# Latent attention: where the causal mask is added, and the order of scores, transposes, exponentials and copies

## The reference, cut to what matters

```python
def one(args):                                   # one block of 128 rows
    q_blk, i = args
    s = jnp.einsum('bhqd,bhkd->bhqk', q_blk, k).astype(jnp.float32) * scale
    qpos = i * Q_BLOCK + jnp.arange(Q_BLOCK)
    s = jnp.where(kpos[None, :] <= qpos[:, None], s, neg)
    p = jax.nn.softmax(s, axis=-1).astype(v.dtype)
    return jnp.einsum('bhqk,bhkd->bhqd', p, v)
```

## Time and profile before

| | |
|---|---|
| median of 3 runs | 1805.03 us (1804.6 to 1806.43) |
| span of the profiled execution | 1807.1 us (it is this execution's only time) |
| TensorE busy | 1759.0 us, 97% of the span |
| VectorE, ScalarE, GpSimd busy | 1087.8, 698.0, 982.2 us |
| first and last turn of latent attention | 602 to 774 us |
| mean granted TensorE clock | 0.993 |

### The profile page before, as it was taken

One profiled execution on the slowest core, in us unless ns is written; L12 is line 12 of the kernel. 1 busy time (PEld: TensorE's weight loads), 2 busy tenths in 40 slices (PEclk: granted clock), 3 DMA queues, 4 the chain that ended last, 5 costly groups with the idle time before them and its releaser, 6 DMA issues.

```text
span 1807.1 us, 25034 instructions
## 1 busy us (share of the span) xinstructions
PE 1759.0 (97%) x8599; PEld 1467.8 (81%) x8599; DVE 1087.8 (60%) x1535; ACT 698.0 (39%) x1243; POOL 982.2 (54%) x554
## 2 busy tenths in 40 slices
PE   7999999999999899999999999999999999999998
PEld 7888888888888677788878888778888888878887
DVE  5655663002334778884345564887777777889842
ACT  7422223111013667731133232644444444444432
POOL 6743333445654577654433232577777777655540
PEclk9999999999999999999999999999999999999999
DMA  6511111347661789583221134243433334494322
GB/s 266 204 52 36 36 43 49 139 164 256 227 227 46 276 317 325 177 308 113 103 71 59 59 104 141 77 139 107 142 117 123 133 110 139 142 344 143 122 76 93
DMA packets 111245, 262.33 MB, mean 145 GB/s; under 512 B 7744, under 2 KB 50368, under 8 KB 106688
## 3 DMA queue, kind: packets, MB, share of 16 engines
q1 hardware_dynamic: 84720, 182.13, 30.3%
q10 hardware_dynamic: 26448, 79.18, 11.8%
HBM read 186.82 MB, written 73.92 MB: 144 GB/s over the span
## 4 chain that ended last, share of the span: by engine, by line
PE 84%; DVE 6%; ACT 5%; issue 2%; DMA 1%; POOL 1%; ACTq 0%; DVEq 0%; SPq 0%; POOLq 0%
PE ps L714 16%; PE ps L719 16%; PE ps L720 16%; PE ps L1333 7%; PE ps L1338 7%; PE ps L1335 7%; PE ps L1408 2%; PE ps L1409 2%; PE ps L1410 2%; ACT prow L1792 2%; PE ps L1110 1%; PE ps L1090 1%; DMA raw<-in_slabs 1%; DVE aneg L2570 1%; PE ps L1431 1%
## 5 line engine op out<-in xcount | busy, mean ns | idle before, releaser
L609 POOL TENSOR_SCALAR wh<-raw 128x1024 fp32r<-128x1024 f32 x75 | 211.6, 2822 | 467.3 <-PE ps L714 448.9
L714 PE MATMUL ps<-uh,wh 128*128 128x512 f32 x560 | 221.2, 395 | 0.7 <-POOL wl L602 0.7
L720 PE MATMUL ps<-uh,wl 128*128 128x512 f32 x560 | 218.4, 390 | 0.0
L719 PE MATMUL ps<-ul,wh 128*128 128x512 f32 x560 | 218.0, 389 | 0.0
L611 POOL TENSOR_TENSOR wl<-raw,wh 128x1024 fp32r<-128x1024 f32 x75 | 182.0, 2427 | 6.3
L646 POOL TENSOR_TENSOR wl<-raw,wh 128x512 fp32r<-128x512 f32 x88 | 137.5, 1573 | 69.1 <-ACT wh L1457 67.8
L633 POOL TENSOR_TENSOR over_rings<-over_rings 128x512 f32<-128x512 f32 x92 | 118.2, 1285 | 51.5 <-DMA over_rings<-in_slabs 45.9
L1457 ACT ACTIVATE wh<-raw 128x512 fp32r<-128x512 f32 (+1 forms) x164 | 105.4, 656 | 88.9 <-PE ps L1338 58.0
L689 POOL TENSOR_TENSOR wl<-raw,wh 128x512 fp32r<-128x512 f32 x63 | 93.7, 1496 | 78.2 <-ACT wh L1457 78.2
L2212 DVE SCALAR_TENSOR_TENSOR ya<-zA,sm,ya 128x512 f32<-128x512 f32 x88 | 109.6, 1246 | 31.7 <-ACT ya L2036 24.6
L720 PEld LDWEIGHTS ps<-uh,wl 128*128 128x128 f32 x560 | 105.1, 188 | 22.6
(11 more groups left out here) (488 smaller groups left out, 4873.9 us busy)
## 6 DMA issues: line engine op xcount, KB each, us to landing
raw<-in_slabs SPq DMA_DIRECT2D x110, 512.0 KB, 3.6
over_rings<-in_slabs SPq DMA_DIRECT2D x22, 1024.0 KB, 7.1
s_s<-over_rings SPq DMA_DIRECT2D x22, 1024.0 KB, 4.9
ssm<-s_s SPq DMA_DIRECT2D x22, 512.0 KB, 4.5
raw<-s_s SPq DMA_DIRECT2D x22, 512.0 KB, 3.8
s_f<-yb ACTq DMA_DIRECT2D x22, 512.0 KB, 5.3
raw<-s_d SPq DMA_DIRECT2D x36, 256.0 KB, 2.5
dsum<-in_slabs SPq DMA_DIRECT2D x16, 512.0 KB, 6.7
```

The source lines that it names most:

```text
L609: pool.tensor_scalar(wh[:, j, :], raw[:, j % RAWS, :], 1.0, None, ALU.mult).then_inc(S["w_hi"], 1)
L714: l = pe.matmul(o, lh, rh, start=start, stop=False)
L719: pe.matmul(o, lh, rl, start=False, stop=False)
L720: return pe.matmul(o, ll, rh, start=False, stop=stop)
```

## The change

The mask leaves TensorE. A tile `maskt` of 1024 columns holds zeros and, in its last 128, the mask. The maximum's pass becomes one VectorE instruction that reads the scores from PSUM and the mask from SBUF, writes minus the masked scores into `prow`, and their minimum into `aneg`. The exponential reads `prow`, with scale -1, and writes it in place. The wait for the transpose of w - 2 moves from the exponential to the maximum, and the scores of w and the first products of the mix wait for the maximum that read their banks, not for the exponential. On TensorE the scores of w + 2 stand ahead of the turn of w; on ScalarE the exponential of w + 1 ahead of the copy of w. VectorE's loop keeps its order. To make room in SBUF the high and low parts are packed: blocks on the diagonal keep 384 columns apart rather than 512 (`turned_at`, `turned_block`), and the tiles move. Two constant tiles and their copies at the start go, and counts of the semaphores that they moved change.

```diff
+DIAG = 3 * P
+
+def turned_at(t, b, n, i):
+    rows = min(CH * (n + 1), i + 1) - CH * n
+    q = i % CH * P
+    if n < b:
+        return t[:, 0:CH * H2].rearrange("p (a n) -> p a n", n=H2)[:, :, q:q + P]
+    each = t[:, CH * H2 * b:CH * H2 * b + 5 * DIAG].rearrange("p (a n) -> p a n", n=DIAG)
+    return each[:, 1:1 + rows, 0:P] if q == DIAG else each[:, 0:rows, q:q + P]
+
+def turned_block(t, b, c, q):
+    at = c * H2 if c < CH * b else CH * H2 * b + (c - CH * b) * DIAG
+    return t[:, at + q:at + H2]
...
-        ident_r = sb("ident_r", [P, P], f32r)
-        mask_r = sb("mask_r", [P, P], f32r)
...
+        (maskt,) = place(157, [("maskt", [P, T], 0)])
...
             def m_scores(w):
                 h, i = UNITS[w]
-                at_least(pe, S["m_exp"], w - 1)
+                at_least(pe, S["m_neg"], w - 1)
...
-                    def mask(o=ps[:, bank, n - P:n]):
-                        pe.matmul(o, ident_r[:, :], mask_r[:, :], start=False, stop=False, skip_group_check=True)
                     l = mm3(ps[:, bank, 0:n], mqh[0:QK, i // CH, q], mql[0:QK, i // CH, q], kh[0:QK, keys],
-                            kl[0:QK, keys], True, True, extra=mask if diag else None)
+                            kl[0:QK, keys], True, True)
...
-                    pe.wait_ge(S["m_exp"], NW - 1 + m)
+                    pe.wait_ge(S["m_neg"], NW - 1 + m)
...
             for w in range(NW):
                 h, r = divmod(w, NT)
+                if w + 2 < NW:
+                    m_scores(w + 2)
                 m_turn(w)
...
-                if w + 2 < NW:
-                    m_scores(w + 2)
                 if w >= CH and w % CH < PV_PARTS:
                     m_pv(w // CH - 1, w % CH)
...
             def m_exp(w):
...
-                if w >= 2:
-                    act.wait_ge(S["m_ptt"], PIECE0[w - 1])
-                act.activation(prow[:, w % 2, 0:n], s2(w)[:, 0:n], ACT.Exp,
+                act.activation(prow[:, w % 2, 0:n], prow[:, w % 2, 0:n], ACT.Exp, scale=-1.0,
...
             for w in range(NW):
                 h, r = divmod(w, NT)
+                if w + 1 < NW:
+                    m_exp(w + 1)
                 m_pth(w)
                 if w > CH and w % CH == PV_PARTS:
                     m_sum(w // CH - 1)
-                if w + 1 < NW:
-                    m_exp(w + 1)
...
-            for o, n in ((ones_r, "ones"), (ident_r, "ident"), (mask_r, "mask")):
-                dve.tensor_copy(o[:, :], cn[:, CN0[n]:CN0[n] + P]).then_inc(S["cst"], 1)
+            dve.tensor_copy(ones_r[:, :], cn[:, CN0["ones"]:CN0["ones"] + P]).then_inc(S["cst"], 1)
...
             dve.memset(krow[:, :, 0:NOPE], 0.0)
+            dve.memset(maskt[:, 0:T - P], 0.0).then_inc(S["o_z"], 1)
...
             def m_max(w):
...
-                dve.tensor_reduce(aneg[:, 0, w % 4:w % 4 + 1], ps[:, c:c + 2, :].rearrange("p a n -> p (a n)")[:, 0:n], AX.X,
-                                  ALU.max, negate=True).then_inc(S["m_neg"], 1)
+                if w >= 2:
+                    dve.wait_ge(S["m_ptt"], PIECE0[w - 1])
+                dve.tensor_tensor_reduce(
+                    prow[:, w % 2, 0:n], ps[:, c:c + 2, :].rearrange("p a n -> p (a n)")[:, 0:n], maskt[:, T - n:T],
+                    -1.0, 3e38, ALU.add, ALU.min, aneg[:, 0, w % 4:w % 4 + 1]).then_inc(S["m_neg"], 1)
...
+            dve.tensor_copy(maskt[:, T - P:T], cn[:, CN0["mask"]:CN0["mask"] + P]).then_inc(S["o_z"], 1)
+            dve.wait_ge(S["o_z"], 2)
             m_max(0)
...
```

More of the change, by code:

```diff
@@ L258, in build @@
         amax, aneg, asum, ainv = (sb(n, [P, 2, CH]) for n in ("amax", "aneg", "asum", "ainv"))
-        sb("line_up_tiles", [P, 80])
+        sb("line_up_tiles", [P, 336])
         ps = ctx.enter_context(nc.psum_tensor("ps", [P, 8, H2], f32))
@@ L290, in build @@
                                              ("qr2", [P, MH, ROPE], 0)])
[L291 to L294, removed]
+        mqh, mql, p0h = place(64, [("mqh", [P, 2, H2], 1), ("mql", [P, 2, H2], 1), ("p0h", [P, 5 * DIAG], 1)])
+        (p0l,) = place(56, [("p0l", [P, 5 * DIAG], 1)])
+        oT, prow, p1h = place(104, [("oT", [P, RH, T], 0), ("prow", [P, 2, T], 0), ("p1h", [P, CH * H2 + 5 * DIAG], 1)])
+        (p1l,) = place(142.5, [("p1l", [P, CH * H2 + 5 * DIAG], 1)])
+        (maskt,) = place(157, [("maskt", [P, T], 0)])
         oth, otl = place(32, [("oth", [P, RH, T], 1), ("otl", [P, RH, T], 1)])
@@ L1073, in m_scores @@
                     bank = 2 + 2 * (w % 2) + c
-                    diag = c == i // CH
                     keys = slice(c * H2, c * H2 + n)
-                    def mask(o=ps[:, bank, n - P:n]):
-                        pe.matmul(o, ident_r[:, :], mask_r[:, :], start=False, stop=False, skip_group_check=True)
                     l = mm3(ps[:, bank, 0:n], mqh[0:QK, i // CH, q], mql[0:QK, i // CH, q], kh[0:QK, keys],
-                            kl[0:QK, keys], True, True, extra=mask if diag else None)
+                            kl[0:QK, keys], True, True)
                 l.then_inc(S["m_s"], 1)
@@ L1108, in m_pv @@
                     c, p = each[k]
-                    qs = slice(max(0, c - CH * b) * P, H2)
-                    l = pe.matmul(ps[:, 1, qs], vr[:, c, h, :, :].rearrange("p a n -> p (a n)"), p[:, c, qs],
+                    q = max(0, c - CH * b) * P
+                    l = pe.matmul(ps[:, 1, q:H2], vr[:, c, h, :, :].rearrange("p a n -> p (a n)"), turned_block(p, b, c, q),
                                   start=k == 0, stop=k == len(each) - 1, skip_group_check=True)
@@ L1778, in o_hi @@
                 copy(oth[:, fb, half(b)], oT[:, fb, half(b)]).then_inc(S["o_hi"], 1)
-            def s2(w):
-                c = 2 + 2 * (w % 2)
-                return ps[:, c:c + 2, :].rearrange("p a n -> p (a n)")
             def m_exp(w):
@@ L1802, in m_pth @@
                     act.wait_ge(S["m_ptt"], q + 1)
-                    copy((p1h if g % 2 else p0h)[:, c0:c1, i % CH * P:(i % CH + 1) * P],
+                    copy(turned_at(p1h if g % 2 else p0h, g % 2, n, i),
                          ps[:, BANK_OF["turn", q], 0:(c1 - c0) * P].rearrange("p (a n) -> p a n", n=P)).then_inc(
@@ L2233, in angle @@
                     dve.tensor_copy(icol[:, :], ps[:, 3, 0:1]).then_inc(S["cst"], 1)
-                    dve.wait_ge(S["cst"], 8)
+                    dve.wait_ge(S["cst"], 6)
                     l = dve.tensor_scalar(ang[:, 0:H2], ps[:, 2, :], icol[:, 0:1], None, ALU.mult)
@@ L2270, in decays @@
                 dve.reciprocal(hx[:, 0, :], xi).then_inc(S["cst"], 1)
-                dve.wait_ge(S["cst"], 10)
+                dve.wait_ge(S["cst"], 8)
                 stt(hx[:, 0, :], hx[:, 0, :], cnc("eps"), hx[:, 0, :], ALU.mult, ALU.mult).then_inc(S["cst"], 1)
@@ L2577, in m_ptl @@
                     c0, c1 = CH * n, min(CH * (n + 1), i + 1)
-                    at = (slice(None), slice(c0, c1), slice(i % CH * P, (i % CH + 1) * P))
                     dve.wait_ge(S["m_pth"], q + 1)
-                    lo((p1l if g % 2 else p0l)[at],
+                    lo(turned_at(p1l if g % 2 else p0l, g % 2, n, i),
                        ps[:, BANK_OF["turn", q], 0:(c1 - c0) * P].rearrange("p (a n) -> p a n", n=P),
-                       (p1h if g % 2 else p0h)[at]).then_inc(S["m_ptl"], 1)
+                       turned_at(p1h if g % 2 else p0h, g % 2, n, i)).then_inc(S["m_ptl"], 1)
             def m_inv(g):
@@ L2685, in clear @@
                 dve.memset(acc_[:, :, :], 0.0).then_inc(S["o_z"], 1)
-                dve.wait_ge(S["o_z"], n + 1)
+                dve.wait_ge(S["o_z"], n + 3)
             def g1_lo(n, h_, gh, gl, gname):
@@ L2843, in _ @@
             dve.memset(zA[:, 0:2], 0.0).then_inc(S["cst"], 1)
-            dve.wait_ge(S["cst"], 12)
+            dve.wait_ge(S["cst"], 10)
             def u_two(i, e):
@@ L2979, in _ @@
             dve.memset(zB[:, 0:2], 0.0).then_inc(S["cst"], 1)
-            dve.wait_ge(S["cst"], 13)
+            dve.wait_ge(S["cst"], 11)
             quarters(0, 0)
```

## The result

The changed kernel takes 1868.38 us (1864.96 to 1870.2, 4 runs) against 1804.86 for the kernel before: 63.5 us more, a ratio of 1.0347 [1.0334, 1.0359]. The profiled execution took 1870.11 us, with a span of 1868.3 against 1807.1, so 61.2 us more by spans. 1863 us was forecast, in 1846 to 1886.

The account below looks back on a forecast made before the run. The prediction took a ScalarE-TensorE ring to bound latent attention, replaced by a closed ScalarE-VectorE lap: 49.3 + 6.4 + 1.9 + 0.3 = 57.9 us on 1805.0 gives 1863 us, range 1846 to 1886.

Parts of the forecast that it names:

- The lap's sum: Latent attention: exponentials, copies, low parts, maxima, hand-overs, output and key work over 64 turns sum to 220.5 us, +49.3 us.
- (b): Maximum's new VectorE pass: reading out its accumulator adds 0.10 us each, 64 times, 6.4 us; ends 0 and 12.5.
- (c): Latent attention's exponential reading SBUF instead of PSUM: +0.03 us each, 64 times, 1.9 us; ends -2 and +4.
- (a): Maximum's new VectorE pass with PSUM and SBUF operands: the old maximum's durations, no change; other end +40 us.
- rival 2: The new VectorE pass runs at the rate of two SBUF operands: +40 us, 1903 us; chance 5%.
- (d): One copy of the mask ahead of the first maximum: 0.3 us; related clearing and start copies -0.5 to +0.5.
- TensorE falls out of the ring: Latent attention: transposes can run a whole lap ahead of their copies, so the mask's 4 us on TensorE count for nothing.
- the rival of the clock and the heads' first scores: TensorE idles some 4 us per head before first scores, its clock falls: 8 to 15 us, about 1874; chance 15%.
- Over long before: On TensorE, scores of w + 2 need the maximum of w, claimed to have finished long before; no size given.
- the stages outside: Sign: stages outside the latent attention, 602 to 774 us, change by no more than 1 us, else the forecast is wrong.
- TensorE's cover: Scores of w + 2 placed first cover the transposes' wait for the exponential, 21.5 us before the change.
- The faster and the even rival: Faster: lap stays open, TensorE bounds, 1785 to 1800 us, 7%. Even: lost and gained cover balance, 1805, 3%.

## Why the prediction came out as it did

**The mechanism held.** The loss stands where the prediction put it: exponential w + 1, copy w, low parts w, maximum w + 2, exponential w + 2. The wait for the maximum is 104.4 us where about 109 us of ScalarE's idle time were to be nearly all of that, and the low parts wait at each of the 64 turns. ScalarE's order alone gives it (+52.7 us), and the maximum's move alone takes it away (-47 us).

**The lap's sum held.** Without (b) the working gives 49.3 + 1.9 + 0.3 = 51.5 us. The kernel with the exponential first, which has that lap and the mask's move but not TensorE's order, measured 52.7, with some 3 us either way; in its trace the stage ends 54.1 us later than before. It held term by term too. Added up by starts over the turns of that trace, it is 50.7 us from an exponential to the copy behind it (the working, with what (c) measured: 47.4 + 2.4), 34.4 from copy to low parts (33.1 and 1.9 of hand-overs), 87.1 from low parts to maximum, with the output and key work between (44.8 + 22.5 + 20.9), and 49.4 from maximum to exponential (46.7, 1.9 of hand-overs and the 0.6 of (b) below).

**(a), the new pass's rate,** came out at the value taken, 1.214 us for 1024 columns where the plain maximum has 1.215, and 0.680 for 512; rival 2, at 1.84 times as long, fell.

**(b), the accumulator, was mis-sized: 6.4 us, where the lap shows 0.6.** By starts, the exponential of 1024 columns follows its maximum after 705.55 - 704.30 = 1.25 us; before it was 656.66 - 655.40 = 1.26. Summed over the 64 turns, from the start of the maximum to the start of its exponential, it is 50.52 us in the changed kernel and 49.96 in that with the new orders and the old mask: 0.6 us for 64 accumulator reads. The Trainium skill, "VectorE: DVE Perf Modes", section "Two Vector instructions with no wait between them", says that an op which also writes out its accumulator is two instructions, the main one and a read. The trace agrees: the read is a second instruction, 64 of 80 ns. What was wrong was to add its time: it starts at 705.44, while the pass, by its row, lasts to 705.50.

**(c), the exponential from SBUF:** 2.4 us, where 1.9 were taken and -2 to 4 allowed. With (b) that makes the 3 us by which the mask's move lengthens the lap, by its rows. **(d)** The mask's copy starts at 601.89 and the first maximum behind it at 602.21 us: 0.32 us, where 0.3 was taken.

**"TensorE falls out of the ring" is the step that failed,** and it is the rival of the clock and the heads' first scores that came true beside the forecast. The new order of TensorE was costed at nothing; it costs 10.8 us on top of the lap by medians (63.5 - 52.7, with some 4 us either way) and 7.6 by the end of the stage in the traces, where that rival had 8 to 15. The working saw the place (the queries' low part, then scores, then the transposes at half clock), but counted it as another case rather than a term. Against the trace with the exponential first, by starts over the turns, the copies come 4.3 us later behind their exponentials and the maxima 2.0 us later behind their low parts. "Over long before" failed as well, as the scores of w + 2 waited 10 times for the maximum of w, 8.7 us in all; but with the heads' first scores behind the turn they still wait 10 times, 8.2 us, and most of the loss is gone, so that wait cost little.

The forecast came nearer than its terms deserved, which is luck: 5.8 us too much for (b) and 7.6 to 10.8 too little for TensorE's order partly cancelled. That the terms now add up to 49.3 + 0.6 + 2.4 + 0.3 + 10.8 = 63.4 us, against the 63.5 measured, proves nothing more, since the 10.8 was itself taken from the 63.5; what could have failed is the lap's own 52.6 against the 52.7 by medians and the 54.1 by the traces. That the array runs at half rate unless lately busy is what the Trainium skill, "TensorE: Matmul & The Clock Gate", Part 1, says. The trace agrees: TensorE was idle until 713.18 us, for 3.03 us, and the granted clock was 0.50 from 714 to 716.

**The other signs.** The last low part ends at 834.8 us, 61.7 later than before, and the span is 61.2 us longer, so the stages outside kept their length within 1 us. That sign is weaker than it was meant to be: from the last low part to the end the thirteen traces of this document have 1028 to 1034 us, though none of the changes touches what stands there. Against the working, TensorE's cover did one thing that it promised, the transposes' wait fell to 1.3 us, and it was worth nothing, since another ring set the pace. The faster and the even rival needed a lap below 2.4 and at 2.7 us per turn; 64 turns in 233 us make 3.6.

## What to carry to other kernels

Where two engines that work in a written order hand each other results, moving a step forward on one of them can close a lap, unless its producer on the other is moved forward by as much: write down the ring of one turn, sum its rows, and compare it with the turn's length before. A wait that a reorder covers is worth nothing if another ring is longer afterwards, and an engine that has fallen out of the ring still belongs in the sum wherever it has its one late input, here seven times, once per head after the first. Here 5.6 us, 0.3%, were to be had by moving maximum and scores forward with ScalarE's order left alone.

## What the runs showed of the hardware

- A VectorE pass that adds an operand from SBUF to one in PSUM, writes the sum to SBUF and returns the row's minimum takes as long as the plain reduction from PSUM: 1.214 us against 1.215 at 128x1024, 0.680 against 0.682 at 128x512.
- Its accumulator read, 80 ns by its rows, delays the reader by 0.6 us in 64 turns, about 0.01 us each: the changed kernel against the one with the new orders and the old mask.
- The exponential with its operand and result in SBUF and a scale of -1 takes 0.037 us longer than from PSUM on average, 0.777 against 0.740; the two were not separated.
- TensorE's granted clock was 0.85 to 0.90 over the stage in the five kernels with the closed lap, 0.91 and 0.92 in the two with the lap open and the scores ahead of the turn, and 0.97 to 0.99 in those with ScalarE's old order and the scores behind the turn. A lower clock cost little where TensorE was off the lap: with the exponential first it was 0.88, and the time was the lap's.
